# Smallest expert group: high and low rows in one operand, experts taken in alternation

## The chip, the cores and the metric

The kernel runs on one NeuronCore of a Trainium2 chip. The metric is the device time of one execution in microseconds, lower is better. The five engines run their own instruction streams and meet at semaphores: TensorE (PE, its weight loads PEld), VectorE (DVE), ScalarE (ACT), GpSimd (POOL) and SyncE (SP), which issues most of the transfers.

## The reference

Two blocks are computed one after the other on 256 rows of 1024 floats. The first has two layers of an attention mixer and a mixture of experts; the second has two layers of gated feed-forward parts and four more mixers. The change touches only the mixture of experts of the first block, twice in an execution:

```
scores = jax.nn.sigmoid((xt @ router_w).astype(jnp.float32))
biased = (scores + router_b.astype(jnp.float32)).reshape(T, N_GROUPS, EXPERTS_PER_GROUP)
group_score = lax.top_k(biased, MOE_TOP_K)[0].sum(-1)
best_group = jnp.argmax(group_score, axis=-1).astype(jnp.int32)
in_group = jnp.take_along_axis(biased, best_group[:, None, None], axis=1)[:, 0]
local = lax.top_k(in_group, MOE_TOP_K)[1]
...
def expert_block(args):
    xi, e = args
    return (jax.nn.silu(xi @ w_gate[e]) * (xi @ w_up[e])) @ w_down[e]
```

There are 16 experts of width 256 in 4 groups of 4. Each of the 256 rows (tokens) goes to one group and to the best two of its experts, weighted by their scores.

## The kernel before

**Precision.** Every product of float32 matrices is made of three TensorE products: each operand is split into a high part (rounded to the engine's format) and a low part (the rest), and `products` (L473 to L478) adds high x high, high x low and low x high in PSUM. ScalarE makes the high parts by a copy, VectorE the low parts by a subtraction. This holds for activations and weights alike; for the experts' weights these are `ex_act_split` (L971) and `ex_dve_split` (L976), one unit of 128x2048 floats (1 MB) at a time.

**Router.** After the scores, each row has a group. TensorE counts the groups (L1031 to L1035), VectorE ranks them (L1095 to L1102) and writes the order as integers for SyncE (`order_i`, L1104), which waits for it before it can load any expert. VectorE then gives each row a place and builds the matrix `spread_s` (L1117), with which TensorE picks the rows of each part out of the 256 (L1044 for the first two parts, `pick_singles`, L1172, for the other three). ScalarE copies the picked rows to `xg`, as high and low. TensorE issues matmuls on zeros in the waits (`pe_warm`, L658).

**Parts and steps.** There are five parts of 128 places. The biggest group has parts 0 and 1, every other group one part. At most one group can have more than 128 rows. `EXPERT_ORDER` lists the experts group by group, and `STEPS` a step for every pair of expert and part: for the big group's four experts two steps each, then twelve experts with one. Each expert has three units of weights: 0 and 1 are gate and up, 2 is down.

**One step** i: TensorE makes the gate and up products (`gates`, 8 x 3 products of 512 columns, into PSUM bank 6), then the down products of step i-1 (`down`, 4 x 3 products), then the transposes of step i's hidden rows (`turn_hidden`, L1197). Meanwhile ScalarE makes the silu (L1268), VectorE multiplies it with the up half and the gates' weight (L1315), and after the transposes ScalarE makes the high part (L1272) and VectorE the low part (L1320). After a group's last expert ScalarE and VectorE copy the sums out (`take_y`, L1279, L1327), and at the end `give_back` adds the parts to the rows.

**Buffers and order.** Units of even experts and of odd experts have a buffer each. SyncE loads them in the order of `SPLIT_ORDER`: from the third expert on, units 0 and 1 wait for the gate products of the last step of the expert before the last (`ex_gates`), unit 2 for its down products (`ex_down`). ScalarE and VectorE make their splits at places written by hand in `act_experts` and `dve_experts`; each engine works its stream in order, so that what stands behind a split waits for its transfer.

## Time and profile before

| | us |
|---|---|
| median of 3 runs | 2104.1 |
| lowest, highest | 2101.69, 2104.67 |
| the profiled execution | 2106.8 |
| its span, first to last instruction | 2105.1 |
| TensorE busy | 2018.7 (96%) |
| VectorE busy | 1331.6 (63%) |
| ScalarE busy | 1009.2 (48%) |
| experts' steps, first layer and second layer | about 360 to 533 and 700 to 873 |

Times in the rows below are microseconds from the first instruction of one profiled execution, unless marked ns. A busy TensorE is not one at its peak: matmuls are pipelined, a row's duration is that of one matmul from start to end, and the next starts earlier. PEclk is the clock granted to TensorE as a share of 2.4 GHz; 0.5 is its lower level.

### The profile page before, as it was taken

The numbers are of one execution on the slowest core, as the hardware profiler recorded it, in microseconds if no ns is written. First come the engines' busy times: TensorE is split into PE (matmuls) and PEld (weight loads), VectorE is DVE, ScalarE is ACT, GpSimd is POOL, SyncE is SP. The second block draws the span as 40 slices with busy tenths as digits, with TensorE's granted clock in tenths as the row PEclk, the third lists the DMA queues.
The fourth block names the chain that finished last, engine by engine and source line by source line (L and its number), as shares of the span: only waits on it lengthen the run. The fifth ranks groups of instructions, "written<-read, shape, count | busy, mean of one in ns | idle before, by whom it ended". The sixth has DMA issues, their size and how long they took to land.

```text
span 2105.1 us, 34303 instructions
## 1 busy us (share of the span) xinstructions
PE 2018.7 (96%) x14362; PEld 1714.0 (81%) x14362; DVE 1331.6 (63%) x1773; ACT 1009.2 (48%) x1142; POOL 21.4 (1%) x36
## 2 busy tenths in 40 slices
PE   8999998999998999999999989999999999889997
PEld 7999986888886887788889776888788799677886
DVE  4554546588887568766754666666666644756665
ACT  3544445476665557644443424444544533425443
POOL 1000000000000000000000000000000000000000
PEclk9999999999999999999999999999999999999999
DMA  7545513498233479645444112555455543104452
GB/s 258 171 151 179 190 68 130 196 375 354 105 110 133 166 281 370 238 171 188 179 180 160 41 63 89 186 197 185 157 197 184 209 151 110 61 3 160 180 193 96
DMA packets 42044, 358.68 MB, mean 170 GB/s; under 512 B 4815, under 2 KB 4959, under 8 KB 8144
## 3 DMA queue, kind: packets, MB, share of 16 engines
q1 hardware_dynamic: 38704, 341.93, 43.8%
q0 software_dynamic: 3232, 15.20, 2.3%
q8 instruction: 82, 1.34, 0.3%
q14 instruction: 26, 0.21, 0.0%
HBM read 355.99 MB, written 1.12 MB: 170 GB/s over the span
## 4 chain that ended last, share of the span: by engine, by line
PE 83%; DVE 7%; ACT 4%; DMA 3%; DVEq 2%; issue 1%; SPq 0%; ACTq 0%
PE psum L784 16%; PE psum L476 15%; PE psum L477 14%; PE psum L478 14%; PE psum L786 8%; DMA ring<-moe_w 3%; PE psum L2561 2%; PE psum L730 1%; PE psum L658 1%; PE psum L1465 1%; DVE ring_lo L976 1%; PE psum L1493 1%; DVE ring_lo L490 1%; PE psum L680 1%; PE psum L1478 1%
## 5 line engine op out<-in xcount | busy, mean ns | idle before, releaser
L490 DVE TENSOR_TENSOR ring_lo<-ring,ring_hi 128x3072 fp32r<-128x3072 f32 (+1 forms) x120 | 398.5, 3321 | 166.9 <-ACT ring_hi L484 166.8
L784 PE MATMUL psum<-xT_both,ring_hi 128*128 128x512 f32 x1408 | 501.3, 399 | 1.7 <-DVE xT_both L600 1.7
L786 PE MATMUL psum<-xT_both,ring_lo 128*128 128x256 f32 x1408 | 395.1, 281 | 0.0
L484 ACT CAST ring_hi<-ring 128x3072 fp32r<-128x3072 f32 (+1 forms) x120 | 327.4, 2730 | 9.8 <-DVE oT L2881 9.5
L784 PEld LDWEIGHTS psum<-xT_both,ring_hi 128*128 128x128 f32 x1408 | 264.5, 188 | 68.8 <-issue 3.5
L786 PEld LDWEIGHTS psum<-xT_both,ring_lo 128*128 128x128 f32 x1408 | 265.9, 189 | 3.1
L478 PE MATMUL psum<-xT_both,ring_lo 128*128 128x256 f32 x896 | 254.1, 284 | 0.0
L976 DVE TENSOR_TENSOR ring_lo<-ring,ring_hi 128x2048 fp32r<-128x2048 f32 x94 | 213.5, 2285 | 38.5 <-ACT ring_hi L971 38.5
L829 ACT COPY scratch<-psum 128x512 f32<-128x512 f32 x88 | 51.8, 588 | 355.0 <-PE psum L786 355.0
L971 ACT CAST ring_hi<-ring 128x2048 fp32r<-128x2048 f32 x94 | 180.1, 1915 | 67.5 <-DMA ring<-moe_w 67.3
L478 PEld LDWEIGHTS psum<-xT_both,ring_lo 128*128 128x128 f32 x896 | 172.6, 193 | 0.0
L476 PE MATMUL psum<-xT_both,ring_hi 128*128 128x256 f32 x512 | 147.7, 288 | 6.4 <-ACT scratch L2186 3.8
L477 PE MATMUL psum<-xT_both,ring_hi 128*128 128x256 f32 x512 | 144.7, 283 | 0.0
L476 PE MATMUL psum<-ring_hi,glu_hi 128*128 128x512 f32 x352 | 138.5, 393 | 0.7 <-DVE glu_lo L864 0.7
L477 PE MATMUL psum<-ring_lo,glu_hi 128*128 128x512 f32 x352 | 138.0, 392 | 0.0
L478 PE MATMUL psum<-ring_hi,glu_lo 128*128 128x512 f32 x352 | 137.0, 389 | 0.0
L476 PE MATMUL psum<-ring_hi,xg 128*128 128x512 f32 x320 | 128.8, 402 | 6.1 <-DVE ring_lo L994 4.5
L478 PE MATMUL psum<-ring_hi,xg 128*128 128x512 f32 x320 | 124.9, 390 | 0.0
L477 PE MATMUL psum<-ring_lo,xg 128*128 128x512 f32 x320 | 124.9, 390 | 0.0
L476 PE MATMUL psum<-xT_both,dil_hi 128*128 128x256 f32 x384 | 111.7, 291 | 0.8 <-ACT scratch L1656 0.8
L1597 DVE TENSOR_TENSOR ring_lo<-ring,dil_hi 128x2048 fp32r<-128x2048 f32 (+1 forms) x31 | 79.4, 2565 | 48.9 <-ACT dil_hi L1673 48.9
L477 PE MATMUL psum<-xT_both,dil_hi 128*128 128x256 f32 x384 | 109.6, 285 | 0.0
(429 smaller groups left out, 3613.7 us busy)
## 6 DMA issues: line engine op xcount, KB each, us to landing
ring<-ff_w SPq DMA_DIRECT2D x88, 1536.0 KB, 6.4
ring<-moe_w SPq DMA_DIRECT2D x94, 1024.0 KB, 6.9
ring<-mix_w SPq DMA_DIRECT2D x20, 1536.0 KB, 6.5
ring<-dil_qk SPq DMA_DIRECT2D x23, 1024.0 KB, 4.9
ring<-proj_w SPq DMA_DIRECT2D x16, 1024.0 KB, 4.9
ring<-dil_v SPq DMA_DIRECT2D x8, 1536.0 KB, 7.0
ring<-sb_w SPq DMA_DIRECT2D x8, 1536.0 KB, 7.6
scratch<-rel_dram POOLq DMA_DIRECT2D x16, 384.0 KB, 4.5
```

Of the source, the lines that this page charges most:

```text
L476: nc.tensor.matmul(dst, w_hi, m_hi, start=start, stop=False, **kw)
L477: nc.tensor.matmul(dst, w_hi, m_lo, start=False, stop=False, **kw)
L478: return nc.tensor.matmul(dst, w_lo, m_hi, start=False, stop=stop, **kw)
L484: nc.scalar.copy(ring_hi[:, s, 0:floats], ring[:, s, 0:floats]).then_inc(high_ready, 1)
L490: nc.vector.tensor_tensor(ring_lo[:, s, 0:floats], ring[:, s, 0:floats], ring_hi[:, s, 0:floats].bitcast(F32), ALU.subtract).then_inc(low_ ...
L784: nc.tensor.matmul(psum[:, bank, :].rearrange("p (w n) -> p w n", w=2), ring_hi[:, s, cols], xT_both[:, :, k, :], start=(k == 0), stop=False)
L786: last = nc.tensor.matmul(psum[:, bank, 0:SEQ], ring_lo[:, s, cols], xT_hi[:, k, :], start=False, stop=(k == KC - 1))
L829: nc.scalar.copy(glu_c[:, b, :, :], psum[:, 2 * b:2 * b + 2, SEQ:2 * SEQ]).then_inc(cross_copied, 1)
L971: nc.scalar.copy(high_flat[:, unit_cols_of(e, u)], ring_flat[:, unit_cols_of(e, u)]).then_inc(high_ready, 1)
L976: nc.vector.tensor_tensor(low_flat[:, cols], ring_flat[:, cols], high_flat[:, cols].bitcast(F32), ALU.subtract).then_inc(low_ready, 1)
L1597: v.tensor_tensor(ring_lo[:, u, 0:n], ring[:, u, 0:n], unit_hi(u).bitcast(F32), ALU.subtract)\
L2561: return pe.matmul(psum[half(o), dst_bank, j * HD:(j + 1) * HD], left[half(o), i, 0:HD], right[half(o), i, 0:HD], start=True, stop=True)
```

## The change

The groups are now ranked fully by size, and parts are dealt by rank: the biggest has parts 0 and 1, the next two have 2 and 3, and the smallest has part 4 (`SMALL`). The smallest of four groups can't have more than 64 of 256 rows, so that the high rows and the low rows of its part are put side by side in one operand of 128 columns. One product with the high weights and one with the low weights then give all that three did: rows 0 to 63 of the result belong to the high activations, rows 64 to 127 to the low ones, and their sum is wanted. For gate and up ScalarE copies rows 64 to 127 down (`fold`) and VectorE adds rows 0 to 63 in two halves; the silu is then read from SBUF. The down products keep both halves, and the matrix that gives rows back takes both.

The order of the experts is changed too: an expert of the biggest group (steps c = 0 and 1) and one of the smallest (c = 4) alternate four times, then come the eight experts of the middle groups. `SPLIT_ORDER` and the hand-written places of the splits follow. 17 warming matmuls stand in the place of 10 after the counts.

```diff
-        EXPERT_ORDER = [(g, j) for g in range(EXPERTS // GROUP) for j in range(GROUP)]
+        EXPERT_ORDER = [(g, j) for j in range(GROUP) for g in (0, SMALL - 1)] + \
+            [(g, j) for g in (1, 2) for j in range(GROUP)]
...
-            [u for e in range(1, N_EX) for u in ([(e + 1, 0), (e + 1, 1)] if e + 1 < N_EX else []) + [(e, 2)]]
+        PAIRED = 2 * GROUP
+        SPLIT_ORDER = [FIRST_HALF] + [(e, u) for e in range(2) for u in range(3)] + \
+            [u for e in range(2, PAIRED, 2) for u in ((e, 0), (e, 1), (e + 1, 0), (e, 2), (e + 1, 1), (e + 1, 2))] + \
+            [(PAIRED, 0), (PAIRED, 1)] + \
+            [u for e in range(PAIRED, N_EX) for u in ([(e + 1, 0), (e + 1, 1)] if e + 1 < N_EX else []) + [(e, 2)]]
...
-            pe_warm(10, 3)
+            pe_warm(17, 3)
...
-            v.tensor_scalar(over, psum[:, 1, 73:76], P + 0.5, None, ALU.is_gt)
...
+            v.tensor_copy(g_size, psum[:, 1, 72:76])
+            v.drain()
...
+            v.tensor_tensor(g_bigger, across(g_size), along(g_size), ALU.is_gt)
+            v.tensor_tensor(g_same, across(g_size), along(g_size), ALU.is_equal)
...
-                            last = pe.matmul(psum[:, 2 * (k % 3) + w, 0:3 * P], rows[:, t, k * P:(k + 1) * P],
+                            last = pe.matmul(psum[:, 2 * (k % 3) + w, 0:SEQ + HD], rows[:, t, k * P:(k + 1) * P],
...
+                    if c == SMALL:
+                        pe.matmul(psum[:, 6, :], x_small[:, k, :], high_flat[:, at:at + 512],
+                                  start=(k == 0), stop=False)
+                        last = pe.matmul(psum[:, 6, :], x_small[:, k, :], low_flat[:, at:at + 512],
+                                         start=False, stop=(k == KC - 1))
+                        continue
...
+                        if c == SMALL:
+                            pe.matmul(psum[:, Y_BANK[c] + h, :], ht_hi[:, n, :], high_flat[:, at:at + 512],
+                                      start=(j == 0 and n == 0), stop=False)
+                            last = pe.matmul(psum[:, Y_BANK[c] + h, :], ht_hi[:, n, :], low_flat[:, at:at + 512],
+                                             start=False, stop=(j == GROUP - 1 and n == 1))
+                            continue
...
+            def fold(i):
+                act.wait_ge(ex_gates, N_STEPS * l + i + 1)
+                act.copy(ex_fold, psum[HD:P, 6, :]).then_inc(ex_fold_parts, 1)
...
+                elif c == SMALL:
+                    high(i - 1)
+                    split(e + 1, 0)
+                    fold(i)
+                    split(e + 1, 1)
+                    silu(i)
...
+                if c == SMALL:
+                    v.wait_ge(ex_fold_parts, 2 * (GROUP * l + j) + 1)
...
+                    v.tensor_tensor(ex_fold[:, gate], ex_fold[:, gate], psum[0:HD, 6, gate], ALU.add).then_inc(ex_fold_parts, 1)
+                    v.tensor_tensor(ex_fold[:, up], ex_fold[:, up], psum[0:HD, 6, up], ALU.add)
+                    v.drain()
+                    v.wait_ge(ex_silued, N_STEPS * l + i + 1)
```

On ScalarE, before, from the high part of the first expert's second step to the second expert's two steps (the L971 are splits, the L1268 silus, the L1272 high parts of the turned hidden rows):

```order
164 L1272 CAST ht_hi<-psum 128x256 [waits ex_turned]
165 L971 CAST ring_hi<-ring 128x2048 [waits ring_full0]
166 L971 CAST ring_hi<-ring 128x2048 [waits ring_full1]
167 L1268 ACTIVATE scratch<-psum 128x256 [waits ex_gates]
168 L971 CAST ring_hi<-ring 128x2048 [waits ex_down_full1]
169 L1272 CAST ht_hi<-psum 128x256 [waits ex_turned]
170 L1268 ACTIVATE scratch<-psum 128x256 [waits ex_gates]
```

After, at the same place, the first expert's second step (row 178) and behind it the small group's first step (L981 are splits, L1306 and L1303 silus, L1298 the fold):

```order
178 L1306 ACTIVATE scratch<-psum 128x256 [waits ex_gates]
179 L981 CAST ring_hi<-ring 128x2048 [waits ex_down_full1]
180 L1313 CAST ht_hi<-psum 128x256 [waits ex_turned]
181 L981 CAST ring_hi<-ring 128x2048 [waits ring_full0]
182 L1298 COPY scratch<-psum 64x512 [waits ex_gates]
183 L981 CAST ring_hi<-ring 128x2048 [waits ring_full1]
184 L1303 ACTIVATE scratch<-scratch 64x256 [waits ex_fold_parts]
185 L1311 CAST ht_hi<-psum 128x2x64 [waits ex_turned]
```

The splits that wait for ring_full0 and ring_full1 are of the third expert now, one expert further on; the small step's silu stands behind both, as the silu of row 167 does, and its fold between them. On VectorE, before, with the multiplies L1315 and the low parts L1320:

```order
278 L1315 SCALAR_TENSOR_TENSOR scratch<-psum,slot_gate,scratch 128x256
279 L1320 TENSOR_TENSOR ht_lo<-psum,ht_hi 128x256
280 L976 TENSOR_TENSOR ring_lo<-ring,ring_hi 128x2048
281 L1315 SCALAR_TENSOR_TENSOR scratch<-psum,slot_gate,scratch 128x256
282 L976 TENSOR_TENSOR ring_lo<-ring,ring_hi 128x2048
```

and after, with the two adds of the fold (L1375, L1376) and the small step's multiply (L1379):

```order
282 L986 TENSOR_TENSOR ring_lo<-ring,ring_hi 128x2048
283 L1392 TENSOR_TENSOR ht_lo<-psum,ht_hi 128x256
284 L986 TENSOR_TENSOR ring_lo<-ring,ring_hi 128x2048
285 L1375 TENSOR_TENSOR scratch<-scratch,psum 64x256
286 L1376 TENSOR_TENSOR scratch<-scratch,psum 64x256
287 L1379 SCALAR_TENSOR_TENSOR scratch<-scratch,slot_gate 64x256
288 L986 TENSOR_TENSOR ring_lo<-ring,ring_hi 128x2048
```

The adds have come in behind the next expert's first low part (row 284) and ahead of its second (row 288). In the router, VectorE's instructions from the counts to the order's cast before:

```order
246 L1095 TENSOR_SCALAR scratch<-psum 128x3
247 L1097 SCALAR_TENSOR_TENSOR scratch<-tab_sb,scratch 128x3
248 L1099 TENSOR_REDUCE scratch<-scratch 128x1
249 L1100 TENSOR_TENSOR scratch<-places,scratch 128x3
250 L1101 TENSOR_TENSOR scratch<-scratch,places 128x3
251 L1102 TENSOR_SCALAR scratch<-scratch 128x1
252 L1104 CAST order_i<-scratch 1x4
```

and after:

```order
246 L1105 COPY scratch<-psum 128x4
247 L1109 TENSOR_TENSOR scratch<-scratch 128x16
248 L1110 TENSOR_TENSOR scratch<-scratch 128x16
249 L1112 TENSOR_TENSOR scratch<-scratch,tab_sb 128x16
250 L1114 TENSOR_TENSOR scratch<-scratch 128x16
251 L1116 TENSOR_REDUCE scratch<-scratch 128x4
252 L1119 TENSOR_TENSOR scratch<-scratch,places 128x16
253 L1120 SCALAR_TENSOR_TENSOR scratch<-scratch 128x4
254 L1122 TENSOR_TENSOR scratch<-scratch,places 128x16
255 L1124 TENSOR_REDUCE scratch<-scratch 128x4
256 L1126 CAST order_i<-scratch 1x4
```

The cast that SyncE waits for stands four instructions further back. Between the first of these rows and the cast VectorE drains three times before the change and eight times after it.

## Rows read from the trace of the kernel before

**Rows 1.** Busy time of each engine by stretch: window, length, busy (count), PEclk, DMA, GB/s

```profile
361.00:427.00 66.00, 66.00 (x299) 54.20 (x298) 35.01 (x33) 29.13 (x29) 0.00 (x0) 1.00 0.51 196
427.00:521.00 94.00, 93.18 (x419) 76.01 (x418) 82.78 (x58) 69.14 (x57) 0.00 (x0) 1.00 0.92 362
...
767.00:862.00 95.00, 92.69 (x413) 74.65 (x413) 83.47 (x58) 69.00 (x57) 0.00 (x0) 1.00 0.90 352
```

**Rows 2.** Waits of TensorE, second layer's single steps: total us, times, longest

```profile
PE psum L1197 <- DVE scratch L1315: 1.3, 3, 0.8
PE psum L476 <- DVE ring_lo L976: 1.0, 3, 0.4
```

**Rows 3.** Timeline of TensorE, 399 to 410: start, us, engine, line, operation

```profile
399.02 0.39 PE L476 MATMUL psum<-ring_hi,ht_hi 128*128 128x512 f32 x1
...
401.75 0.38 PE L1197 MATMUL psum<-tab_sb,scratch 128*128 128x128 f32 x2
401.88 0.48 PE L476 MATMUL psum<-ring_hi,xg 128*128 128x512 f32 x1
...
407.44 0.39 PE L476 MATMUL psum<-ring_hi,ht_hi 128*128 128x512 f32 x1
...
410.16 0.38 PE L1197 MATMUL psum<-tab_sb,scratch 128*128 128x128 f32 x2
```

**Rows 4.** Timeline of TensorE, end of the first layer's picks

```profile
359.54 0.44 PE L1197 MATMUL psum<-tab_sb,scratch 128*128 128x128 f32 x2 [1.68 <-DVE scratch L1315]
```

**Rows 5.** Timeline of ScalarE, 399 to 409

```profile
399.22 0.38 ACT L1268 ACTIVATE scratch<-psum 128x256 f32<-128x256 f32 x1 [4.08 <-PE psum L478]
...
404.11 1.91 ACT L971 CAST ring_hi<-ring 128x2048 fp32r<-128x2048 f32 x1 [1.57 <-DMA ring<-moe_w]
406.60 1.92 ACT L971 CAST ring_hi<-ring 128x2048 fp32r<-128x2048 f32 x1 [0.58 <-DMA ring<-moe_w]
```

**Rows 6.** Timeline of VectorE, 399 to 412

```profile
399.64 0.48 DVE L1315 SCALAR_TENSOR_TENSOR scratch<-psum,slot_gate,scratch 128x256 f32<-128x256 f32 x1 [1.68 <-ACT scratch L1268]
...
406.05 2.29 DVE L976 TENSOR_TENSOR ring_lo<-ring,ring_hi 128x2048 fp32r<-128x2048 f32 x1 [3.06 <-ACT ring_hi L971]
...
409.23 2.28 DVE L976 TENSOR_TENSOR ring_lo<-ring,ring_hi 128x2048 fp32r<-128x2048 f32 x1
```

**Rows 7.** Groups by line and shape, whole span: count, busy, mean ns, idle before

```profile
L829 ACT COPY scratch<-psum 128x512 f32<-128x512 f32 x88 | 51.8, 588 | 355.0 <-PE psum L786 355.0
L831 ACT ACTIVATE scratch<-scratch 128x256 f32<-128x256 f32 x88 | 36.9, 419 | 48.1 <-DVE scratch L855 48.1
...
L855 DVE TENSOR_TENSOR scratch<-psum,scratch 128x256 f32<-128x256 f32 x88 | 37.4, 424 | 111.3 <-ACT scratch L829 110.8
```

**Rows 8.** Landing times of the experts' units, second layer, 701 to 767

```profile
DMA to landing us min/median/max: 4.9/6.9/9.9
```

**Rows 9.** Timeline of VectorE in the first layer's router

```profile
332.99 0.16 DVE L1095 TENSOR_SCALAR scratch<-psum 128x3 f32<-128x3 f32 x1 [0.45 <-PE psum L1035]
333.22 0.16 DVE L1097 TENSOR_TENSOR_SCAN scratch<-tab_sb,scratch 128x3 f32<-128x3 f32 x1
...
333.89 0.16 DVE L1104 CAST order_i<-scratch 1x4 int32<-1x4 f32 x1
...
334.90 1.02 DVE L1117 TENSOR_SCALAR spread_s<-places,scratch 128x640 fp32r<-128x640 f32 x2
```

**Rows 10.** The same engine a little later, an operation on 32 elements

```profile
337.62 0.19 DVE L1138 TENSOR_TENSOR scratch<-scratch 128x32 f32<-128x32 f32 x1
```

**Rows 11.** The chain that ended last, first layer, 330 to 350

```profile
336.17 8.19 DMA ring<-moe_w
344.39 1.92 ACT ring_hi L971
...
346.33 2.30 DVE ring_lo L976
...
348.68 0.50 PE psum L476
```

**Rows 12.** Landing time of the unit issued at 756.6

```profile
DMA to landing us min/median/max: 8.0/8.0/8.0
```

**Rows 13.** Busy time by stretch, columns as in Rows 1

```profile
695.00:699.00 4.00, 4.00 (x16) 4.00 (x15) 3.90 (x3) 3.02 (x5) 0.00 (x0) 0.57 0.00 0
```

**Rows 14.** Timeline of TensorE, second layer's single steps

```profile
837.28 0.44 PE L1197 MATMUL psum<-tab_sb,scratch 128*128 128x128 f32 x2 [0.77 <-DVE scratch L1315]
```

125 lines of the change are left out of this document (85 added, 40 removed).

## The prediction

> **What bounds the kernel now.** I read the table of busy time first: TensorE is busy for 96% of the span, so the question is not which engine but where TensorE gives time away. The change touches only the experts' part of each of the two layers, so I cut that part into stretches. In the stretch of the big group's steps TensorE runs 299 matmuls and transposes in 66 us without a pause while the DMA engines are half busy; in the stretch of the twelve single steps it runs 419 in 94 us in the first layer and 413 in 95 us in the second, with the DMA engines 90 to 92% busy [rows 1]. So each group's steps cost what TensorE needs for their products, and the single steps lose a little besides, on ScalarE's and VectorE's work [rows 2]. The transfers keep up throughout, with no time to spare in the single steps and much in the big group's.
>
> The timeline of TensorE gives the price of a product. A down product group of 12 starts at 399.02, the transposes at 401.75, the next 24 gate products at 401.88, the next down group at 407.44, the next transposes at 410.16 [rows 3]: 2.72/12 = 0.227 us for one product of 512 columns, 5.56 us for a step's gate products, 0.14 for the transposes. The 0.39 us that a row shows as one matmul's duration is latency and is not paid 24 times.
>
> **What the change removes.** A step of the smallest group has 16 gate products instead of 24 and 8 down products instead of 12: 12 x 0.227 = 2.72 us fewer, in 4 steps of 2 layers: 8 x 2.72 = **21.8 us**, all on TensorE's path. The Trainium skill, page "TensorE: Matmul & The Clock Gate", section "Back-to-back issue gap", gives about 131 ns as the sustained spacing of 512-column matmuls; by it the removed work would be 96 x 0.131 = 12.6 us, and the whole sum below would come to about -0.5 us. The rows of this very stream say 0.227, and the measurement decides.
>
> The pick of the single parts streams 320 columns instead of 384. It saves nothing: TensorE waits 1.68 us for VectorE after those matmuls, before the first transposes at 359.54 [rows 4], and the first of them run while it waits for weights. ScalarE copies the picks in two pieces instead of one; 8 small copies more, under the same cover. The transposes of 64 rows, and the splitting of hidden activations over half the columns, are gains under 0.1 us a step and I count them as nothing.
>
> **What it moves: the wait that takes the place of the products.** Until now a single step followed a single step; now each small step S stands between a big group's second step B and the next expert's first step A. The weights for that A go into the buffers that B's gate products free. So the time from the end of B's gate products to S's hidden activations is a chain of transfer, splits and S's own work, because ScalarE and VectorE are given the next expert's splits ahead of S's. I walk one period with the rows of the second step of the third expert, whose gate products end at 399.02 and after which the same unit is loaded and split today.
> - TensorE: A's down products 399.02 to 401.75, B's transposes, then S's 16 gate products from 401.88 to 405.63 (5.56 less 8 x 0.227), then B's 12 down products, 2.72, to 408.35. TensorE could turn S's hidden rows at **408.35**.
> - ScalarE: the unit is there and its high part starts at 404.11, 1.91 us [rows 5]. S's fold (a copy of 64x512 out of PSUM; 0.59 us as for the 128x512 one [rows 7]) waits for the gates (405.8) and for this split (406.0), so it ends at 406.6, just as the second unit's split starts at 406.60. That one ends at 408.52.
> - VectorE: the low part of the first unit starts at 406.05, 2.29 us, to 408.34 [rows 6]. Only behind it stands S's first add of the folded halves: 0.42 us [rows 7], starting 0.08 before the split's end, to 408.68.
> - ScalarE then makes the silu out of SBUF: 0.42 us [rows 7], 408.72 to 409.14. VectorE multiplies: 0.48 [rows 6], 409.18 to 409.66. TensorE turns at **409.72**.
>
> The pause is 409.72 - 408.35 = 1.37 us; the second add (0.42) and the fold lie beside this chain. Eight of them: **+11.0 us**. Queued behind the late multiply on VectorE is the second unit's low part, 409.6 to 411.9; the next A wants it after 12 gate products, 409.86 + 2.78 = 412.6: no second wait, with 0.7 us of room. Behind the silu on ScalarE stands only the high part of S's turned rows, which is wanted a whole gate group later. In the next A, TensorE covers silu and multiply (about 1.1 us) with S's 8 down products (1.8 us), and the small expert's units, issued after S's and B's groups, have 20 us. So there is one pause a period and not more. Bounds: the three short operations have not run in this form; at 0.37 to 0.48 us each they move the pause by 0.2 us either way, and a longer landing moves it one to one: units took 4.9 to 9.9 us to land in the second layer's big-group stretch, by their place in the queue [rows 8]. I take 1.37 and keep 0.9 to 2.4.
>
> **The router.** The new ranking has ten steps from its first instruction to the order's cast, eight of them behind a drain; the old one has six, three of them behind a drain. The old cast starts 0.90 us after its first instruction (332.99 to 333.89), the first drained step costs 0.23 [rows 9], and an operation on 32 elements in this stage is 0.03 us longer than one on 3 [rows 10]. With 0.25 for a drained step and 0.10 for an undrained one the new cast starts 8 x 0.25 + 2 x 0.10 = 2.2 us after it, +1.3 us (1.1 to 1.5). On SP the first experts' loads wait for this cast, and they are the path: the unit issued at 336.17 lands 8.19 us later and the first step's fifth product waits for it [rows 11]. The spread matrix comes 1.1 later (one drained step fewer behind the cast) and hides under that. The seven more warming matmuls on TensorE end before it. Two layers: **+2.6 us**. Moving expert units (1,2) ahead on SP costs nothing, since its transfer lands long before the third step.
>
> **Fewer single steps in a row.** Twelve become eight. At the big-group rate of 66/299 = 0.2207 us an instruction, the single stretches lose 94 - 92.5 and 95 - 91.2, together 5.3 us [rows 1]; a third less is 1.8, nothing less is the other bound. I take **-1.5 us**.
>
> **Sum**: -21.8 + 11.0 + 2.6 - 1.5 = **-9.7 us**. The profiled execution took 2106.8 us (span 2105.1), which would become 2097.1. The median of the runs shown is 2104.1, 2.7 less, and the same difference gives **2094.4 us**.
>
> **The rivals.**
> 1. *The pause is smaller or absent* (0.12). If S's adds got ahead of the splits or units landed faster, the gain would be -21.8 + 2.6 - 1.5 = -20.7: 2083.4. Against it: every link but three short ones has a row in just this order. A pause halved gives 2089.
> 2. *The pause is larger* (0.20). S's silu also stands behind the second unit's high part, with 0.2 us to spare. In the second layer one such unit took 8.0 us instead of 6.7 to 6.9 [rows 12]. That late in every period, the silu comes 1.0 us later: +8, 2102.4; in some of them, 2098 to 2102.
> 3. *The other side: TensorE's clock* (0.07). The trace shows the half level once in this part: granted clock 0.57 of full over 695 to 699, a loss of 4 x 0.43 = 1.7 us, after a router stage with many short pauses [rows 13]. If each of the eight pauses brought such a stretch, 13.7 us are lost and the result is 2108.1; one more in the first layer's router, 2109.8. It needs six to eat the gain, eight or nine to be slower by 0.2%. Against it: after the wait before the transposes at 837.28 (0.77 us) the clock stayed full [rows 14], and the new pauses stand 24 us apart. The Trainium skill, page "TensorE: Matmul & The Clock Gate", section "A second HAM failure mode: psum-queue depth-cycling", tells of a kernel in which frequent micro-idles between matmul groups made the clock oscillate; by it this rival would be the outcome, and that row speaks for a full clock.
> 4. *The change doesn't do what it says* (0.05): if the pairs of products that share a stationary operand were spaced 3/2 as wide, S would be as long as before and have no pause. Only router and single steps are left: 2105.2. No row speaks for it.
>
> **How the numbers follow.** The forecast (0.56) covers pauses of 1.0 to 1.8 us: 2091 to 2098. A measurement of this kernel tells a change from none at about 0.2%, 4.2 us. Faster: the forecast, rival 1 and the lower part of rival 2, 0.56 + 0.12 + 0.06 = 0.74. Within 0.2%: the rest of rival 2 (0.14), rival 4 (0.05), part of rival 3 (0.02): 0.21. Slower: 0.05. The range 2087 to 2103 leaves out half of rival 1 and rivals 3 and 4, 0.18 together.
>
> **What the changed profile would show.** Gate products of S spaced 0.227 us, 16 of them; a wait of TensorE before S's transposes, on VectorE's multiply, eight times, shown as about 1.2 us of idle each (a row's latency covers the rest); none elsewhere in a period; cast of the order 2.2 us after the ranking's first instruction; PEclk at 1.0 through the alternation. Wrong would be: waits before A's fifth product (the second unit came late), no waits at all, a spacing other than 0.227, or a clock of 0.5 behind the pauses.

## The result and the profile after

| | kernel before | changed kernel |
|---|---|---|
| median of the first comparison, 14 runs each | 2104.5 us | 2101.6 us |
| ratio of the two | | 0.9974 (0.9962 to 0.9987) |
| the same two kernels in a second comparison | 2105.1 (29 runs) | 2100.9 (12 runs), ratio 0.9978 (0.9965 to 0.9990) |
| the profiled execution | 2106.8 | 2097.2 |

The change makes the kernel faster, by 0.26%: 5.5 us by the ratio (2.7 to 8.0), where -9.7 was forecast. 2094.4 was forecast for the median and 2101.6 came, inside the range of 2087 to 2103, though outside the band of 2091 to 2098 that the forecast itself covered. The two profiled executions differ by 9.6 us, almost exactly the forecast, and that must not be read as a proof: single executions of the kernel before lie between 2097 and 2114 us, so one pair can be further off than the whole change is large. One execution of the kernel before (4002.8 us) and one of fold_first (3286.7 us) were disturbed and are left out of all means below.

The table of busy time by stretch, for the changed kernel: window, length, busy time of TensorE, of its weight loads, of VectorE, of ScalarE and of GpSimd with their counts, the granted clock, the DMA share, GB/s. The first and third rows answer to the big group's steps in [rows 1] (now the big and the small group in turns), the others to the single steps.

```profile
361.00:427.00 66.00, 62.14 (x276) 50.05 (x276) 46.11 (x43) 36.59 (x36) 0.00 (x0) 1.00 0.69 249
427.00:517.00 90.00, 87.97 (x392) 71.01 (x392) 74.23 (x56) 62.52 (x54) 0.00 (x0) 1.00 0.84 326
700.00:766.00 66.00, 62.34 (x280) 50.37 (x279) 47.26 (x44) 37.08 (x35) 0.00 (x0) 1.00 0.71 266
766.00:853.00 87.00, 85.22 (x381) 68.72 (x380) 72.15 (x54) 61.62 (x53) 0.00 (x0) 1.00 0.84 324
```

TensorE was busy through all 66 us before, in both layers; now it is idle for 3.9 and 3.7 of them, although the clock is full (three of each layer's four small steps lie in those rows). The table of waits says what it waits for. First line: first layer, 361 to 450; second line: second layer, 700 to 800 (total us, times, longest):

```profile
PE psum L1223 <- DVE scratch L1379: 5.1, 4, 1.3
```

```profile
PE psum L1223 <- DVE scratch L1379: 5.0, 4, 1.4
```

L1223 is the transposes of the hidden rows, L1379 the multiply of the folded step. Four such waits in each layer, and no other in the alternation. The timeline of TensorE in the period that the forecast walked (start, us, engine, line, operation; in brackets the idle time before and who ended it):

```profile
392.62 0.38 PE L1223 MATMUL psum<-tab_sb,scratch 128*128 128x128 f32 x2
392.75 0.48 PE L1209 MATMUL psum<-ring_hi,xg 128*128 128x512 f32 x1
393.07 0.40 PE L1211 MATMUL psum<-ring_lo,xg 128*128 128x512 f32 x1
...
396.52 0.39 PE L480 MATMUL psum<-ring_hi,ht_hi 128*128 128x512 f32 x1
...
399.02 0.39 PE L482 MATMUL psum<-ring_hi,ht_lo 128*128 128x512 f32 x1
400.60 0.33 PE L1223 MATMUL psum<-tab_sb,scratch 64*128 64x64 f32 x2 [1.20 <-DVE scratch L1379]
400.87 0.50 PE L480 MATMUL psum<-ring_hi,xg 128*128 128x512 f32 x1
...
408.25 0.38 PE L1223 MATMUL psum<-tab_sb,scratch 128*128 128x128 f32 x2
```

And of ScalarE and VectorE over the same time, the links of the chain in their order:

```profile
395.03 1.91 ACT L981 CAST ring_hi<-ring 128x2048 fp32r<-128x2048 f32 x1 [1.63 <-DMA ring<-moe_w]
396.97 0.58 ACT L1298 COPY scratch<-psum 64x512 f32<-64x512 f32 x1
397.51 1.92 ACT L981 CAST ring_hi<-ring 128x2048 fp32r<-128x2048 f32 x1
399.62 0.42 ACT L1303 ACTIVATE scratch<-scratch 64x256 f32<-64x256 f32 x1 [0.19 <-DVE scratch L1375]
```

```profile
396.97 2.29 DVE L986 TENSOR_TENSOR ring_lo<-ring,ring_hi 128x2048 fp32r<-128x2048 f32 x1 [2.04 <-ACT ring_hi L981]
399.18 0.41 DVE L1375 TENSOR_TENSOR scratch<-scratch,psum 64x256 f32<-64x256 f32 x1
399.51 0.41 DVE L1376 TENSOR_TENSOR scratch<-scratch,psum 64x256 f32<-64x256 f32 x1
400.07 0.48 DVE L1379 SCALAR_TENSOR_TENSOR scratch<-scratch,slot_gate 64x256 f32<-64x256 f32 x1 [0.15 <-ACT scratch L1303]
```

Read together: the unit lands at 395.03, its high part runs to 396.94, its low part to 399.2, and only then come the folded step's add, the silu and the multiply. TensorE started its last product at 399.02. Where nothing has to be waited for (the version halves below) the transposes of a small step start 0.32 us behind that, here at 399.34; they started at 400.60, 1.26 us later.

In the router (timeline of VectorE) the cast of the order now starts 2.13 us after the ranking's first instruction, for 0.90 in [rows 9]:

```profile
330.60 0.16 DVE L1105 COPY scratch<-psum 128x4 f32<-128x4 f32 x1 [0.44 <-PE psum L1045]
...
332.73 0.16 DVE L1126 CAST order_i<-scratch 1x4 int32<-1x4 f32 x1
```

### The profile page after: what moved, and what is told of

It is laid out like the page before. It is cut to its first block, busy times and chain, and to the rows that moved or that the text cites. A ratio compares the mean times of both kernels' runs of the same rounds, so it can differ in the third digit from the quotient of the medians.

```text
span 2095.5 us, 34189 instructions
## 1 busy us (share of the span) xinstructions
PE 1996.7 (95%) x14268; PEld 1693.5 (81%) x14280; DVE 1337.7 (64%) x1795; ACT 1011.2 (48%) x1166; POOL 21.3 (1%) x36
## 4 chain that ended last, share of the span: by engine, by line
PE 78%; DVE 8%; DMA 5%; ACT 5%; DVEq 2%; issue 1%; SPq 0%; ACTq 0%
PE psum L788 16%; PE psum L480 14%; PE psum L481 13%; PE psum L482 13%; PE psum L790 8%; DMA ring<-moe_w 4%; PE psum L2643 2%; DVE ring_lo L986 1%; PE psum L734 1%; ACT ring_hi L981 1%; PE psum L662 1%; DVE ring_lo L494 1%; PE psum L1547 1%; PE psum L1575 1%; PE psum L1560 1%
## 5 line engine op out<-in xcount | busy, mean ns | idle before, releaser
L788 PEld LDWEIGHTS psum<-xT_both,ring_hi 128*128 128x128 f32 x1408 | 264.5, 188 | 68.7 <-issue 3.5
L981 ACT CAST ring_hi<-ring 128x2048 fp32r<-128x2048 f32 x94 | 179.7, 1912 | 46.5 <-DMA ring<-moe_w 46.4
L480 PE MATMUL psum<-ring_hi,xg 128*128 128x512 f32 x256 | 104.6, 409 | 4.9 <-DVE ring_lo L1004 4.2
L859 DVE TENSOR_TENSOR scratch<-psum,scratch 128x256 f32<-128x256 f32 x88 | 37.3, 424 | 111.7 <-ACT scratch L833 111.2
L480 PEld LDWEIGHTS psum<-xT_both,ring_hi 128*128 128x128 f32 x512 | 97.9, 191 | 7.8 <-issue 7.6
```

The costliest lines, as they stand in the source:

```text
L480: nc.tensor.matmul(dst, w_hi, m_hi, start=start, stop=False, **kw)
L788: nc.tensor.matmul(psum[:, bank, :].rearrange("p (w n) -> p w n", w=2), ring_hi[:, s, cols], xT_both[:, :, k, :], start=(k == 0), stop=False)
L981: nc.scalar.copy(high_flat[:, unit_cols_of(e, u)], ring_flat[:, unit_cols_of(e, u)]).then_inc(high_ready, 1)
```

## The experiments

### How the runs are compared

Each run lists TensorE's mean granted clock over the execution, and time follows it. Fitted through the 109 runs of the kernel before, a run is 1.5 us longer for each 0.001 of mean clock that it lacks, and the kernels below give 1.1 to 1.8. So the table gives two numbers beside the median: the mean of that clock, and the mean time brought to a clock of 0.993 with each kernel's own line ("at equal clock" below). The second compares the instruction streams, the first says what the clock adds. The runs of all comparisons are pooled here; the standard error of a mean of 12 is about 0.9 us and 0.0005 of clock, that of the changed kernel's 26 is 0.6 and 0.0003, that of the kernel before 0.35 and 0.0002.

| kernel | runs | median us | mean clock | mean us at 0.993 |
|---|---|---|---|---|
| before | 109 | 2105.6 | 0.9930 | 2105.0 |
| changed | 26 | 2101.3 | 0.9907 | 2097.1 |
| alt_only | 12 | 2105.7 | 0.9928 | 2105.3 |
| rank_alone | 11 | 2106.9 | 0.9923 | 2106.5 |
| old_order | 12 | 2106.0 | 0.9913 | 2104.1 |
| fold_first | 11 | 2105.0 | 0.9894 | 2101.0 |
| busy_pause | 12 | 2100.8 | 0.9911 | 2097.5 |
| warm | 12 | 2098.1 | 0.9930 | 2098.2 |
| before_warm | 12 | 2104.5 | 0.9933 | 2105.8 |
| halves (two sets of six) | 12 | 2088.8 | 0.9922 | 2087.5 |
| best | 5 | 2091.3 | 0.9920 | 2088.9 |

**Theory A** is the prediction's: the folded products are gained in full, and a pause set by the chain of landing, splits and the step's own operations gives half of it back. Its rivals changed as results came in; theories C to H are named in the expectations.

### after_again and before_again: what repeats

No edit to either kernel.

> The changed kernel, unaltered, to learn which numbers repeat. The forecast's sum (21.8 us of products removed, eight pauses of 1.4 us and 2.6 us of ranking added) says 9.7 us less than the kernel before, and so did the pair of profiled executions (2106.8 to 2097.2), while the runs said 5.5 us less (2.7 to 8.0). If the sum is right and the first runs were an unlucky draw, the new runs give about 9.7 us less, and the profile again shows TensorE's wait on the line of the second add of the folded step at about 1.4 us x4 in each layer. Rival: something the sum lacks costs about 4 us in most executions; then the runs again give 5 to 6 us less and the profile shows where, in stretches at the half clock level near the router stage (two in the first profile, at 341 and 358 us, none there before) or elsewhere.

> The kernel before, unaltered, as the measure of what differs between equal kernels. Expected: a ratio of 1.000, a profiled execution of 2104 to 2107 us, and the segments of the experts' stage (order cast to first transposes, the steps of each layer) within 1 us of the first profile of it; half-level stretches at other places than in the first profile if they are chance, at the same places if the program sets them.

Measured: 2100.9 us, ratio 0.9978 (0.9965 to 0.9990), and 2106.1 us, ratio 0.9997 (0.9984 to 1.0011). The smaller gain repeats, so the 9.6 us between the two first profiled executions was a draw. The wait on the multiply is there again, and it is the same in both layers:

```profile
PE psum L1223 <- DVE scratch L1379: 5.1, 4, 1.4
```

What does not fit the forecast is the clock: 0.9907 over the 26 runs of the changed kernel, 0.9930 before. At equal clock the two kernels are 7.9 us apart, close to the sum; 0.0023 x 1.5 us per 0.001 = 3.5 us is taken by the clock. So the sum was nearly right about the instruction stream, and something that it priced at nothing costs 3.5 us on average.

### halves and halves_again: the pause taken away

In each alternation the next big-group expert's two gate units are split in halves, and the folded step's operations stand between them (the waits of TensorE and the order of units follow; VectorE's is shown, ScalarE's is alike with both halves of the first unit ahead of fold and silu).

```
                 elif c == SMALL:
-                    split(e + 1, 0)
+                    ex_dve_part(e + 1, 0, 0)
                     hidden(i)
-                    split(e + 1, 1)
+                    ex_dve_part(e + 1, 0, 1)
+                    ex_dve_part(e + 1, 1, 0)
+                    ex_dve_part(e + 1, 1, 1)
```

> One edit to the changed kernel: in each alternation the next big-group expert's two gate units are copied high and subtracted low in halves, as the layer's first unit already is, and the fold's adds, the silu and the multiply stand between the low halves in place of behind a whole unit. Theory A (the pause is the chain landing, high part 1.91, low part 2.29, then add, silu, multiply): the multiply ends about 1.5 us earlier, before TensorE is done with the down products, and TensorE waits under 0.2 us before the small step's transposes; 8 x 1.4 = 11 us less than the changed kernel, about 2090.5 us, and none of it comes back before the next expert's products, since their second half is ready about 0.6 us early. Rival B (the pause is the folded step's own four operations, 0.58 + 0.42 + 0.42 + 0.48 us, in a row, wherever they stand): the pause stays above 1 us and the time within 3 us of the changed kernel. Rival C (the halves' extra 16 instructions and their overheads on ScalarE and VectorE push the next expert's products back): the pause goes from the transposes to the next expert's first or third product, and the time is 0 to 5 us less.

Measured: 2086.6 us, ratio 0.9903 (0.9882 to 0.9924). VectorE in the second set's profile, at the same place of the program:

```profile
395.38 1.22 DVE L1003 TENSOR_TENSOR ring_lo<-ring,ring_hi 128x1024 fp32r<-128x1024 f32 x1 [1.19 <-ACT ring_hi L998]
396.94 0.41 DVE L1396 TENSOR_TENSOR scratch<-scratch,psum 64x256 f32<-64x256 f32 x1 [0.33 <-ACT scratch L1317]
397.27 0.41 DVE L1397 TENSOR_TENSOR scratch<-scratch,psum 64x256 f32<-64x256 f32 x1
397.84 0.48 DVE L1400 SCALAR_TENSOR_TENSOR scratch<-scratch,slot_gate 64x256 f32<-64x256 f32 x1 [0.16 <-ACT scratch L1322]
398.24 3.48 DVE L1003 TENSOR_TENSOR ring_lo<-ring,ring_hi 128x1024 fp32r<-128x1024 f32 x3
```

The four short operations take as long as before; only what stands ahead of them is half as long. The multiply starts 2.46 us after the low part does (3.10 before the edit), and that low part itself starts a half unit sooner behind the landing. TensorE does not wait at all:

```profile
361.00:427.00 66.00, 66.00 (x297) 53.51 (x296) 48.50 (x51) 39.59 (x43) 0.00 (x0) 1.00 0.71 263
```

Rivals B and C of that expectation fall. A small step takes 6.69 us from transposes to transposes where it took 8.0, 1.3 us less, in seven of eight cases (the last one of the second layer took 7.0 here, and 7.6 in the first set's profile). The median came out about 4 us below what that gives, with a mean clock of 0.993 in those six runs. That disagreed with theory E (the router stage costs the clock, see warm below), which had formed meanwhile, so the same kernel ran again:

> The version with halved units once more, unaltered, since its first six runs (2086.6 us, mean clock 0.9933) stand against theory E. Its router stage is that of the changed kernel, and only the pauses are gone. Theory E (the router stage of the changed kernel costs 0.0025 of mean clock): the first six were a lucky draw; the mean clock comes to 0.991 and the median to 2089 to 2091 us, and the profile shows two or three pieces at half level between 335 and 362 us. Theory H (the clock's loss comes with the pauses, or with what they do to the steps behind, though filling them with products of zeros did not bring it back): mean clock 0.993 again, 2085 to 2088 us, and at the same clock 10 us less than the changed kernel. Either way the time is at least 14 us below the kernel before, and the pauses' own 1.3 us each are gone.

Measured: 2091.0 us, ratio 0.9923 (0.9902 to 0.9944), mean clock 0.9912: theory E's time and clock and not H's, but one piece at half level from 335 to 362 us (at 343 to 346), where E asked for two or three. The two sets of six differ by 0.0021 of clock, twice the error of that difference, and nothing was changed between them. Over all twelve the clock is 0.9922, which is above the changed kernel's 0.9907 by about twice its error too: that the first six were only a lucky draw fits E, but it is not shown, and these runs alone don't exclude that the pauses take a part of the clock. The version stands at 2088.8 us over all twelve and, at equal clock, 9.6 us below the changed kernel and 17.5 below the kernel before. With best, from which it can't be told apart, it is the fastest kernel of the study.

### alt_only and rank_alone: the parts without the fold

alt_only runs the smallest group's step as any other (a constant FOLDED, which is None, takes the place of SMALL where the folded operand is made and used), and keeps alternation and ranking. rank_alone goes back to experts group by group as well.

```
-                    if c == SMALL:
+                    if c == FOLDED:
```

> The alternation, the ranking of the groups by size and the order of the units alone; the smallest group's step is again a whole step with separate high and low operands (48 + 24 products instead of 32 + 16 at the gates and half that at the down products), and its columns are picked with 384 columns. Theory A: 8 x 12 products of 0.227 us come back (+21.8) and the eight pauses of 1.4 us go (-11.4), since the step no longer has its adds and its products end 3.6 us later than the buffers come free: 10.4 us more than the changed kernel, about 2107 to 2112 us, in one band with the kernel before plus 1.1 us (ranking +2.6, single steps -1.5). Rival: the alternation itself costs or brings something that the sum gave as nothing; then the time stands more than 3 us from the kernel before's 2104.5 plus 1.1.

Measured: 2105.7 us, ratio 0.9998 (0.9982 to 1.0015), 2105.3 at equal clock: 8.2 us above the changed kernel (with an error of about 1), where 10.4 was expected, and below the expected range of 2107 to 2112 us. (The products of a small step are 24 + 12 for 16 + 8; the expectation's 48 and 32 are twice that, its 8 x 12 is right.) The pauses are gone, as expected; all that TensorE waits for between 363 and 450 is:

```profile
PE psum L1224 <- DVE scratch L1384: 0.7, 2, 0.4
```

So fold and pauses together are worth 8.2 us. With 1.33 us for each pause (the mean of the first profile's eight, against transposes 0.32 us behind the last product; 10.6 together) the fold's products are worth 8.2 + 10.6 = 18.8 us by the runs, not 21.8. The profiles say where the rest is: three steps (big, big, small) take 25.25 us before and 22.82 in the version without pauses, 2.43 less and not 2.72. Around the small step's transposes, of 64x64, TensorE needs more than around those of 128x128. In halves_again:

```profile
391.64 0.40 PE L482 MATMUL psum<-ring_hi,ht_lo 128*128 128x512 f32 x1
391.88 0.38 PE L1242 MATMUL psum<-tab_sb,scratch 128*128 128x128 f32 x2
392.01 0.48 PE L1228 MATMUL psum<-ring_hi,xg 128*128 128x512 f32 x1
...
398.24 0.39 PE L482 MATMUL psum<-ring_hi,ht_lo 128*128 128x512 f32 x1
398.56 0.34 PE L1242 MATMUL psum<-tab_sb,scratch 64*128 64x64 f32 x2
398.83 0.50 PE L480 MATMUL psum<-ring_hi,xg 128*128 128x512 f32 x1
```

From the last down product to the next gate product 0.37 us with full transposes, 0.59 with those of 64 rows: 0.22 us each time, 1.8 us in all. The other 0.07 us a period lie in the neighbouring steps.

> The kernel before with only the ranking of the four groups by size (and its longer filler on TensorE, 17 products of zeros for 10): experts group by group, every step whole, the smallest group last. Theory E (the router stage of the changed kernel costs the clock): the time is the forecast's 2.6 us above the kernel before, and the mean clock falls from 0.993 to 0.991, which costs another 3 us: 2109 to 2111 us, with stretches at half level at 342 and 356 us. Rival F (ranking costs only its own length, and the clock's loss needs the folded steps or the alternation): mean clock 0.993, 2106.5 to 2108.5 us. Rival G (the ranking's length is hidden): within 1 us of the kernel before.

Measured: 2106.9 us, ratio 1.0010 (0.9996 to 1.0024), mean clock 0.9923: nearer to rival F than to E, and in F's range by the time. At equal clock it is 1.5 us above the kernel before, with an error of about 0.8; the two profiles' casts, 1.23 us later in each layer, say 2.5. Alternation without the fold is then 1.2 us below rank_alone, which fits the -1.5 for fewer single steps in a row and is no larger than the error. Its share in the loss of clock is 0.0007, a third of the whole and little more than its error.

### fold_first: the order on the two engines decides who waits

```
                 elif c == SMALL:
-                    split(e + 1, 0)
                     hidden(i)
+                    split(e + 1, 0)
                     split(e + 1, 1)
```

(and on ScalarE the silu ahead of the second unit's high part.)

> The changed kernel with one thing moved: the folded step's copy, adds, silu and multiply stand ahead of the next expert's first gate unit on both engines, not between its parts. Theory A (the pause is a chain, and what stands first on ScalarE and VectorE decides who waits): the wait ahead of the small step's transposes is gone, and TensorE waits for the next expert's first low part instead, 1.5 to 2.3 us (fold 0.58, add 0.42, silu 0.42, multiply 0.48 ahead of a unit split of which 1.91 and 2.29 are then still to come, less the 1.4 us by which the unit's load lands later than the gates end); the time within 4 us above the changed kernel, 2101 to 2106 us. Rival B (the fold's own operations are the pause): their place in the order changes nothing, the wait stays ahead of the transposes at 1.4 us.

Measured: 2105.2 us, ratio 1.0006 (0.9990 to 1.0022); at equal clock 3.9 us above the changed kernel. The wait left the transposes for the next expert's first product (waits of TensorE, 361 to 450, and its timeline):

```profile
PE psum L480 <- DVE ring_lo L986: 4.8, 3, 1.7
```

```profile
401.46 0.50 PE L480 MATMUL psum<-ring_hi,xg 128*128 128x512 f32 x1 [1.52 <-DVE ring_lo L986]
```

Small step 6.7 us, next step 9.2 to 9.5 instead of 7.66 (11.0 in two cases, see below). Theory A holds and B falls: ahead of the unit's splits the same four operations cost the small step nothing, and they delay the next expert's first low part instead. A pause is there because two chains share the engines behind one late landing. Only where the splitting is finer (halves) do both fit.

This is also the one kernel in which the clock fell in the alternation. The pause of 1.61 us ahead of the product at 425.95 was followed by a stretch at half level, and the same step in the second layer by another (table of stretches, the eighth column is the granted clock):

```profile
420.00:427.00 7.00, 5.39 (x25) 4.10 (x25) 4.53 (x5) 5.23 (x6) 0.00 (x0) 1.00 0.85 301
427.00:431.00 4.00, 4.00 (x12) 3.16 (x11) 3.59 (x3) 1.42 (x1) 0.00 (x0) 0.57 0.98 406
...
768.00:772.00 4.00, 4.00 (x12) 3.16 (x11) 4.00 (x3) 1.71 (x1) 0.00 (x0) 0.58 1.00 416
```

Two of its eight pauses did that, those of 1.61 and 1.62 us; behind the longer ones, up to 1.74, the clock stayed full. Its mean clock is the lowest of all, 0.9894.

### busy_pause: are the pauses what costs the clock?

```
             def turn_hidden(i):
+                if STEPS[i][0] == SMALL:
+                    pe_warm(6, 7)
                 pe.wait_ge(ex_hidden, N_STEPS * l + i + 1)
```

> One edit to the changed kernel: six products of zeros (0.23 us each, 1.4 us) stand on TensorE ahead of the wait for each small step's multiply, so that TensorE works through the eight pauses and everything else begins when it did. The runs so far: the mean granted clock is 0.9932 over 40 runs of the kernel before, 0.9907 over 26 of the changed one, 0.9933 over 6 of the version without pauses, and a run is 1.5 us longer for each 0.001 of it. Theory C (the pauses make the clock fall more often, here or in the stages behind): with the pauses filled the mean clock goes back to 0.993 and the median falls by 3 to 4 us to 2097 to 2098 us, though no operation got shorter. Rival D (the clock's loss has another cause, such as the router stage or where later stages fall): the mean clock stays at 0.9907 and the median within 1.5 us of 2101.3, or a little above where a filler runs past the end of the pause.

Measured: 2100.8 us, ratio 0.9977 (0.9961 to 0.9992), mean clock 0.9911 with an error of 0.0004: rival D. TensorE is busy through the pause, and the steps last as long as before (8.0 to 8.1 us for a small one):

```profile
401.12 1.24 PE L662 MATMUL psum<-zero 128*128 128x512 bf16 x5
```

The clock did not come back, so the idleness of the pauses is not what costs most of it. Theory C falls for the changed kernel.

### warm and before_warm: the router stage

```
+            pe_warm(8, 6)
             gates(0)
             slot_gates_of()
             pick_singles(range(3, KC))
+            pe.wait_ge(picked_copied, 2 * KC * l + KC + 6)
+            pe_warm(8, 4)
             turn_hidden(0)
```

> Two groups of eight products of zeros added to TensorE in the router stage of the changed kernel, one ahead of the first gate products (it idles there 2.1 us) and one ahead of the first transposes of the hidden rows (it idles there 2.3 us); the eight pauses stay. The stretches at half level that both profiles of the changed kernel show there are at 341 to 342 us, 356 to 358 us and 697 us. Theory C (the pauses of the alternation cost the clock): the mean clock stays near 0.991 and the median within 1.5 us of 2101.3. Rival E (the router stage of the changed kernel costs it): these stretches go, the mean clock comes to 0.993 and the median falls by 3 to 4 us. If the kernel before has those stretches as often, a gain of 1.7 us for each that goes is had whatever the alternation does.

Measured: 2098.1 us, ratio 0.9967 (0.9952 to 0.9983), mean clock 0.9930, as theory E asks; at equal clock it is 1.1 us above the changed kernel, so that the gain is the clock's. The stretch from 335 to 363 us (first layer's loads, first gates and picks) in the two profiles of the kernel before, then in the two of the changed kernel, then in warm:

```profile
335.00:363.00 28.00, 22.20 (x129) 19.39 (x129) 14.37 (x26) 21.20 (x25) 0.00 (x0) 1.00 0.48 188
```

```profile
335.00:363.00 28.00, 24.75 (x132) 21.63 (x131) 14.43 (x20) 21.02 (x25) 0.00 (x0) 0.94 0.45 181
```

```profile
335.00:363.00 28.00, 23.39 (x126) 19.87 (x125) 13.81 (x22) 21.02 (x33) 0.00 (x0) 0.88 0.57 225
```

```profile
335.00:363.00 28.00, 24.55 (x127) 21.67 (x127) 12.87 (x23) 21.20 (x33) 0.00 (x0) 0.82 0.58 226
```

```profile
335.00:363.00 28.00, 24.75 (x143) 19.63 (x144) 13.84 (x27) 21.03 (x33) 0.00 (x0) 1.00 0.58 226
```

1.00 and 0.94 before; 0.88 and 0.82 changed; 1.00 with the fillers. What TensorE waits for in that stretch of the changed kernel, from its timeline:

```profile
340.69 0.50 PE L480 MATMUL psum<-ring_hi,xg 128*128 128x512 f32 x1 [2.01 <-DVE ring_lo L1004]
...
358.48 0.69 PE L1223 MATMUL psum<-tab_sb,scratch 128*128 128x128 f32 x2 [2.21 <-DVE scratch L1383]
```

The second of these waits was 1.68 in [rows 4]. rank_alone, which has the new ranking and the pick of 384 columns, shows 1.68 there too. So the 0.53 us more goes with the fold's narrower pick (320 columns): the products end earlier, VectorE doesn't, and the saved work is idleness. The first wait, too, is longer in the first layer: it was 1.51 us in the profile of the kernel before, and it is 1.68 in rank_alone and 1.98 in alt_only, which have no fold. (In the second layer it is 1.48 us in both kernels.)

How the clock went with these waits in the profiles with no fillers in this stage. The last column adds up the clock lost over 330 to 365 and 665 to 705 us, the router stages of both layers (each 5 us slice times what its granted clock lacks to 1):

| profile | wait ahead of the first gate product, first layer | half level within 2 us behind it | lost in both router stages |
|---|---|---|---|
| before, before_again | 1.51, 1.53 us | no, no | 1.7, 1.7 us |
| rank_alone | 1.68 | no | 0 |
| busy_pause, halves | 1.65, 1.68 | no, no | 3.4, 3.4 |
| old_order | 1.78 | yes | 6.9 |
| after_again, fold_first | 1.87, 1.87 | yes, yes | 6.8, 6.8 |
| alt_only | 1.98 | yes | 6.8 |
| the changed kernel | 2.01 | yes | 3.4 |
| halves_again | 2.09 | yes | 3.5 |

The wait of 2.2 us ahead of the first transposes stands nine times in these profiles, in either layer, and seven times the clock fell behind it; where it was 1.68, four times (the kernel before and rank_alone), it never fell. So the clock fell more often behind both waits that grew, and the first of them needs no fold: alt_only lost as much here as any. They are not the whole of it, since some stretches at half level had no wait right ahead of them (in before_again at 352 us). Outside the router stages the four profiles of the two kernels lost 14.7 and 16.0 us (before) and 14.7 and 14.7 (changed): the difference between the kernels lies in this stage. One profile is not a mean: alt_only's has the lowest clock of its twelve runs, and over all of them it lost hardly more than the kernel before.

> The kernel before with the two groups of eight products of zeros in its router stage, as in the version of the changed kernel that came to 2098.1 us (3.2 us less, mean clock 0.9930 for 0.9907). If the changed kernel lost clock there that the kernel before did not lose, this one gains nothing: 2104.5 to 2106 us, mean clock 0.993. If the gain is one that any of the kernels has for the taking, the mean clock rises to 0.995 and the time falls by 2 to 3 us, to about 2102.5 us; the changed kernel's own loss is then to be sought elsewhere.

Measured: 2104.5 us, ratio 0.9998 (0.9985 to 1.0012), mean clock 0.9933 for 0.9930. The same fillers give the kernel before nothing. So warm gave back something that the changed kernel had lost and the kernel before had not, and the profiles place it in the router stage.

### old_order: the fold without the alternation

```
-        EXPERT_ORDER = [(g, j) for j in range(GROUP) for g in (0, SMALL - 1)] + \
-            [(g, j) for g in (1, 2) for j in range(GROUP)]
+        EXPERT_ORDER = [(g, j) for g in range(EXPERTS // GROUP) for j in range(GROUP)]
```

> The folded small group without the alternation: experts group by group as in the kernel before, the smallest group last, its four folded steps in a row. A folded expert takes TensorE 5.7 us but its three units of weights 7.4 us of the queue at the rate of the single steps. Theory A: the four small steps become bound by their weights; three periods between them are 7.4 to 8.5 us instead of 8.41 (the first still covered by units ahead), so of the 21.8 us of products at most 6 to 8 us are kept over both layers, less 2.6 us of ranking: 2100 to 2104 us, with TensorE waiting for low parts whose releaser is a landing. Rival: units that were loaded early cover more than one step, and the products' whole 10.9 us a layer are gained without the pauses: 2086 to 2090 us, and the alternation was not needed.

Measured: 2106.0 us, ratio 1.0006 (0.9988 to 1.0024); at equal clock 2.4 us (with an error of a little over 1) below rank_alone, its counterpart without the fold. That is above theory A's 2100 to 2104 us, and the reason in that expectation was only half right. In each layer the four small steps come 9.5, 8.1 and 6.6 us apart, where 7.4 to 8.5 was expected. The profile shows VectorE, not the queue alone, at its limit between the second and the third, 8.1 us apart:

```profile
508.67 4.47 DVE L982 TENSOR_TENSOR ring_lo<-ring,ring_hi 128x2048 fp32r<-128x2048 f32 x2
513.07 0.41 DVE L1365 TENSOR_TENSOR scratch<-scratch,psum 64x256 f32<-64x256 f32 x1
513.40 0.41 DVE L1366 TENSOR_TENSOR scratch<-scratch,psum 64x256 f32<-64x256 f32 x1
513.96 0.47 DVE L1369 SCALAR_TENSOR_TENSOR scratch<-scratch,slot_gate 64x256 f32<-64x256 f32 x1 [0.15 <-ACT scratch L1305]
514.36 2.28 DVE L982 TENSOR_TENSOR ring_lo<-ring,ring_hi 128x2048 fp32r<-128x2048 f32 x1
516.56 0.28 DVE L1379 TENSOR_TENSOR ht_hi<-psum,ht_hi 128x128 fp32r<-128x128 f32 x1
```

Three low parts and the step's own four operations fill it from 508.67 to 516.76. A step whose products are cut to two thirds has the same three units to split, so it is only worth as much as its neighbours' steps give VectorE room. That is what the alternation is for, and it is the part of the change that turns the fold's 2.4 us into 8.2, or, without the pauses (halves against alt_only), 17.8.

### best: everything that helped, together

halves and warm, and in the router one key for the ranking:

```
-            v.tensor_copy(g_size, psum[:, 1, 72:76])
+            v.scalar_tensor_tensor(out=g_size, in0=psum[:, 1, 72:76], scalar=4.0, in1=places[:, K_IOTA:K_IOTA + 4],
+                                   op0=ALU.mult, op1=ALU.subtract)
```

with the second comparison and its two drained steps gone.

> The halved units, the two groups of zero products in the router stage, and the ranking with one key (size times four less the place, so that equal groups need no second comparison; two drained VectorE steps fewer a layer), together. Expected from the parts: 2086.6 us for the halved units alone, less 1 to 1.4 us for the ranking, less 1.7 us for each stretch at half level that goes from the router stage (the profile of the halved version has one at 359 and one at 694 us): 2082 to 2085 us, mean clock 0.994 to 0.995, the cast of the order 0.5 to 0.7 us sooner after the router's first instruction (2.13 us in the changed kernel). Rival: the phase at which the stages fall decides the clock more than the fillers do; then the mean clock stays at 0.993 and the time at 2085 to 2087 us.

Measured: 2091.3 us of five runs (2086.3 to 2094.2), ratio 0.9921 (0.9900 to 0.9943), mean clock 0.9920. The expectation missed. Its parts are in the trace: the cast of the order starts 1.55 us after the ranking's first instruction, 0.58 less than in the changed kernel,

```profile
330.82 0.16 DVE L1122 SCALAR_TENSOR_TENSOR scratch<-psum,places 128x4 f32<-128x4 f32 x1 [0.44 <-PE psum L1062]
...
332.37 0.16 DVE L1139 CAST order_i<-scratch 1x4 int32<-1x4 f32 x1
```

and the clock is full from 335 to 363. But the gain of 2 to 3 us in all is hardly larger than the error of a mean of five runs, 1.5 us, and the clock was lost elsewhere (in the second layer's router stage at 686 to 689 us, and 0.77 over 1150 to 1165 us, a stage that no edit touches). From halves it can't be told apart.

## Why the prediction was right, and where it was off

- **TensorE is the bound, a product costs 0.227 us.** Right. The folded step's products are spaced as all others (rows from 392.75 on: 0.32 for the first, 0.23 after it). Rival 4 (no gain from the fold) is out: three steps are 2.43 us shorter.
- **Products removed, -21.8.** Mis-sized: 8 x 2.43 = -19.4 us. The line that went wrong is the one that counted the transposes of 64 rows as a small gain: they are a loss of 0.22 us a step, 1.8 of the missing 2.4 us. The spacing of 131 ns that the Trainium skill gives in "TensorE: Matmul & The Clock Gate", section "Back-to-back issue gap", would have made the fold 12.6 us; the trace of the changed kernel disagrees with it as that of the kernel before did.
- **The pause, 1.37 us x 8 = +11.0.** Right in mechanism, place, number and nearly in size: 1.2 to 1.4 us of idle in each, 1.33 on average against a turn without a wait, +10.6. The links measured 1.91, 2.29, 0.41, 0.42 and 0.48, for the 1.91, 2.29, 0.42, 0.42 and 0.48 of the working. halves and fold_first show that it is this chain. No second wait in a period: right.
- **Router, +2.6.** The cast came 2.13 us after the ranking's first instruction, forecast 2.2: +1.23 a layer, +2.5. rank_alone's runs say +1.5 with an error of 0.8.
- **Single steps, -1.5.** Borne out by rank_alone against alt_only (-1.2), but within the error.
- **Sum.** -19.4 + 10.6 + 2.5 - 1.5 = -7.8; the runs at equal clock say -7.9. The last two terms are measured to about 1 us only, so that the agreement to 0.1 is luck; that the sum holds within 1 to 2 us is what the runs show.
- **The clock, priced at nothing in the sum and at 0.07 as rival 3.** This is the step that failed. 3.5 us went here, and between the pooled medians only 4.3 us are left of the 7.9. The rival put a loss behind the eight pauses; with the pauses filled (busy_pause) the clock stayed at 0.9911, and in both profiles it was full from the second step of the alternation to its end. warm and the profiles show the loss in the router stage, which the prediction walked only for the length of the ranking. The sentence "it saves nothing", of the narrower pick, was right about time and overlooked that saved work under a wait is a longer wait; and the wait ahead of the first layer's first gate product, which grew also in kernels without the fold, does not appear in it at all. The Trainium skill, page "TensorE: Matmul & The Clock Gate", section "A second HAM failure mode: psum-queue depth-cycling", speaks of frequent micro-idles between groups of matmuls that make the clock oscillate: eight pauses of 1.2 to 1.4 us, 24 us apart, did not; of fold_first's, 1.5 to 1.7 us long, two of eight were followed by a fall.
- **The time in its range.** 2101.6 us lies where the prediction had put rival 2, a larger pause (2098 to 2102), and the pause was not larger. The range held by its width and not by the forecast.
- **Open.** Which part of the change costs how much of the 0.0023. The kernels with the new ranking but without the fold have 0.9925 (23 runs), those with the fold and no fillers in the router stage 0.989 to 0.992. So the runs point at the fold's part of this stage, and yet alt_only's one profile shows the same loss without it. Ranking, the narrower pick and ScalarE's second copy all stand in that stage, and one of them alone was tried only in rank_alone. Nor can one say from these runs why the stretches at half level of the later stages come and go between executions of one kernel.

## What to carry to other kernels

When work is taken from the bound engine, the step that got shorter still has all its transfers and splits: look at which engine has room beside it, and place the shortened step next to steps that give that room (here that turned 2.4 us into 8.2). The new wait is then likely a chain behind a late landing; cutting the long operations ahead of the short ones in halves is cheap, and it was worth at least as much as the change itself (9.6 us against 7.9). And look at the mean clock beside the time: 3.5 of this change's 7.9 us were hidden by a clock loss of 0.0023, in a stage that the prediction had priced for its length only.

## What the runs showed of the hardware

- The mean granted clock of single executions of one and the same kernel (the one before) runs from 0.990 to 0.997, and each 0.001 is 1.5 us. That explains a part of the scatter of single runs; beside it some 2 us are left.
- From the start of the last product ahead of two transposes to the start of the next behind them TensorE took 0.59 us where these were of 64x64, and 0.37 where they were of 128x128 (halves_again, no wait in between).
- Filling the idle time of the router stage with products of zeros brought the mean clock back from 0.9907 to 0.9930 in the changed kernel; filling the pauses of the alternation did nothing for it (0.9911), and in the kernel before the same fillers moved it by 0.0003.
- The length of a pause did not decide by itself whether the clock fell behind it: in fold_first it fell behind 1.61 and 1.62 us and not behind 1.71 and 1.74, and in the router stages behind seven of nine waits of 2.2 us.
- ScalarE's copy of 64x512 out of PSUM took 0.58 us, as long as one of 128x512 [rows 7], and the 64x256 operations took 0.41 to 0.42, as those of 128x256 (0.42): half the partitions saved nothing here.
